# Decode attention of a hybrid decoder step: value pages become the stationary operand in full fp32

## The reference

```python
s = einsum('bqhcd,bkhcd->bhcqk', q, k_all) * ATTN_SCALE      # c: two halves of 64
p = softmax(s over the 1024 past and 4 new tokens)
w = p[:, :, 0] - lam * p[:, :, 1]                             # (8 heads, 4 queries, tokens)
out = einsum('bhqk,bkhe->bqhe', w, v_all)                     # per head: 4 queries x 128
```

## Time and profile before

| what | value |
|---|---|
| median of the runs | 1901.7 us |
| the profiled execution | 1898.74 us, its span 1896.6 us |
| decode, keys of sequence 0 (from the first transpose) | 1485.2 to 1510.7 us |
| decode, seven turns | 1510.7 to 1748.4 us |
| decode, values of sequence 7 | 1748.4 to 1774.3 us |
| output phase | 1778.7 to 1896.6 us |
| PE busy, mean granted clock over the span | 90%, 0.94 |

### The profile page before, as it was taken

How to read it: one execution, slowest core, us unless ns; L and a number is a source line. 1 busy time by engine, 2 the same in 40 slices (tenths; PEclk the granted TensorE clock), 3 DMA queues, 4 the chain that set the end, 5 groups by cost and what they waited for, 6 DMA issues and landing times. The chain is left out here.

```text
span 1896.6 us, 31172 instructions
## 1 busy us (share of the span) xinstructions
PE 1703.2 (90%) x9243; PEld 1384.7 (73%) x9243; DVE 1042.4 (55%) x2696; ACT 839.5 (44%) x1994; POOL 320.4 (17%) x814
## 2 busy tenths in 40 slices
PE   4299999999999997997999999999999588887798
PEld 3287887878788785777878778778788466665476
DVE  4534445444443444344777767767766466676443
ACT  5244434333343332243555545555545366665322
POOL 1011212212121120010122221221222012111101
PEclk8699999999999997998999999999999789898799
DMA  5123050340413103132211211211100567767713
GB/s 154 36 56 72 22 92 2 90 81 11 92 14 78 27 11 135 52 129 63 61 56 40 65 50 42 58 54 44 39 23 26 200 228 259 272 227 237 263 58 110
DMA packets 164757, 171.97 MB, mean 91 GB/s; under 512 B 14634, under 2 KB 133834, under 8 KB 164658
## 3 DMA queue, kind: packets, MB, share of 16 engines
q1 hardware_dynamic: 161538, 170.78, 30.6%
q10 hardware_dynamic: 3120, 0.01, 0.1%
HBM read 141.85 MB, written 28.91 MB: 90 GB/s over the span
## 5 line engine op out<-in xcount | busy, mean ns | idle before, releaser
L1016 PE MATMUL PS<-WH,XH 128*128 128x512 f32 x512 | 212.5, 415 | 0.0
L1016 PE MATMUL PS<-WH,XL 128*128 128x512 f32 x512 | 201.9, 394 | 0.0
L1016 PE MATMUL PS<-WL,XH 128*128 128x512 f32 x512 | 201.9, 394 | 0.0
L1997 PE MATMUL PS<-W,XH 128*128 128x512 f32 x384 | 123.8, 403 | 0.0
L2423 PE MATMUL PS<-cst,RAW 128*128 128x128 f32 x512 | 87.3, 322 | 40.5 <-DVE XL L2330 34.9
L1751 ACT ACTIVATE WORK<-PD,WORK 128x896 f32<-128x896 f32 (+7 forms) x128 | 94.9, 741 | 62.7 <-DVE WORK L1918 57.6
L1016 PEld LDWEIGHTS PS<-WH,XL 128*128 128x128 f32 x512 | 96.2, 188 | 22.8
L2423 PEld LDWEIGHTS PS<-cst,RAW 128*128 128x128 f32 x512 | 68.5, 165 | 58.7 <-DVE XL L2330 42.6
L1016 PEld LDWEIGHTS PS<-WH,XH 128*128 128x128 f32 x512 | 96.7, 189 | 19.8
L1016 PEld LDWEIGHTS PS<-WL,XH 128*128 128x128 f32 x512 | 96.8, 189 | 17.1
L2330 DVE TENSOR_TENSOR XL<-PS,XH 128x512 fp32r<-128x512 f32 x128 | 83.9, 684 | 38.2 <-ACT XH L2251 38.1
(11 more groups left out here) (361 smaller groups left out, 4575.4 us busy)
## 6 DMA issues: line engine op xcount, KB each, us to landing
RAW<-in_cache_k SPq DMA_DIRECT2D x64, 512.0 KB, 4.7
WORK<-in_cache_v SPq DMA_DIRECT2D x64, 512.0 KB, 4.6
RAW<-in_w_in_a SPq DMA_DIRECT2D x40, 512.0 KB, 7.0
out<-WORK SPq DMA_DIRECT2D x16, 512.0 KB, 3.0
out<-RAW SPq DMA_DIRECT2D x16, 512.0 KB, 3.2
RAW<-in_w_in_b SPq DMA_DIRECT2D x60, 128.0 KB, 2.3
RAW<-in_w_kv SPq DMA_DIRECT2D x56, 128.0 KB, 2.3
WORK<-d_G SPq DMA_DIRECT2D x8, 528.0 KB, 12.1
```

The lines of the kernel that those rows point to most:

```text
L1016: last = nc.tensor.matmul(bank, x[:, k, tok(t, P)], wkvoz(w)[:, k, :], start=(k == i == 0), stop=(k == KT - 1 and i == 2))
L1997: last = nc.tensor.matmul(out, x[:, k, at(NT - 1 - s)], w[:, k, cols], start=(k == i == 0), stop=(k == KT - 1 and i == 2))
```

## The change

The values are no longer split. A page of values in plain fp32 is the stationary operand, 128 x 128 per head, and the moving operand is that head's four columns of `WS`. `OUT` is now 128 x 32 (turned: a column per query), is copied into `OT` once per turn, and after the last sequence eight transposes bring `OT` back, straight into the row block of `X1` that the output phase reads. `d_av`, its stores and the 16 reads are gone, and so are `AVS`, `WTS`, `VH`, `VL` and GpSimd's part. Values have six slots, of which pages 4 and 6 share one, and 5 and 7 another. The transposes of keys go round four banks, and `W` takes its place in that round. `PE_ORDER` and `ORDER` are new. The page table is loaded in an earlier phase, and the first loads of keys no longer wait for `pre`.

```diff
-            VB = take(4, D)
+            V_SLOT = (0, 1, 2, 3, 4, 5, 4, 5)
+            VB = take(6, D)
-            OUT = PD[0]
-            ORDER = ("Q", "K0", "E", "K1", "K2", "K3", "V0", "W", "K4", "V1", "R0", "V2", "K5", "V3", "K6", "V4",
-                     "R1", "V5", "V6", "K7", "V7", "L")
-            PE_ORDER = ("T0", "T1", "T2", "T3", "S0", "T4", "W", "S1", "T5", "V0", "V1", "V2", "T6", "S2", "V3", "T7",
-                        "V4", "V5", "V6", "S3", "V7", "N")
+            OUT = BK[4][:, 0:H * DS]
+            TURNS = [u for u in range(10)] + ["W"] + [u for u in range(10, 16)]
+            T_BANK = {u: BK[(0, 1, 7, 5)[n % 4]] for n, u in enumerate(TURNS)}
+            ORDER = ("Q", "K0", "E", "K1", "K2", "K3", "K4", "W", "R0", "K5", "K6", "K7", "R1", "L")
+            PE_ORDER = ("T0", "T1", "T2", "S0", "T3", "T4", "W", "S1", "V0", "T5", "V1", "V2", "T6", "V3", "V4", "T7",
+                        "S2", "S3", "V5", "V6", "V7", "N")
...
                     def values(i, p):
+                        if p < 4:
+                            wait(sp, av, PAGES * (i - 1) + p + 1)
+                        elif p < 6:
+                            wait(sp, av, PAGES * (i - 1) + p + 3)
+                        else:
+                            wait(sp, av, PAGES * i + p - 1)
...
                         def value(p):
-                            for j in range(2):
-                                for w in (VH, VL):
-                                    x = nc.tensor.matmul(OUT[0:64, j, :], WTS[:, p, :], w[p % 4][:, 512 * j:512 * j + 512],
-                                                         start=(p == 0 and w is VH), stop=False)
+                            pe.wait_ge(v_ld[V_SLOT[p]], 16 * (i + 1) if p < 4 else 16 * (2 * i + (p - 2) // 2))
+                            if p == 0:
+                                pe.wait_ge(wr, i + 1)
+                                wait(pe, avc, i)
+                            apart(pe)
+                            for h in range(H):
+                                x = nc.tensor.matmul(OUT[:, h * DS:(h + 1) * DS], VB[:, V_SLOT[p], h * P:(h + 1) * P],
+                                                     WS[:, p * TS + h * DS:p * TS + (h + 1) * DS],
+                                                     start=(p == h == 0), stop=False)
...
                     sequences(pe, body)
+                    pe.wait_ge(avc, DB)
+                    pe.wait_ge(wr, DB)
+                    for h in range(H):
+                        x = nc.tensor.transpose(BK[h // 4][0:TS, (h % 4) * P:(h % 4 + 1) * P], OT[:, h, :], ident)
```

More of the change, by code:

```diff
@@ L2176, in keys, with values, turn @@
                           .then_inc(k_ld[p % 4], 16)
[L2178 to L2185, removed]
-                        src = cache_v[page(sp, i * PAGES + p), :, :, :]
[L2187 to L2201, removed]
+                    def values(i, p):
+                        if p < 4:
[4 more added lines that the diff above has]
+                            wait(sp, av, PAGES * i + p - 1)
+                        src = cache_v[page(sp, i * PAGES + p), :, :, :]
+                        sp.dma_start(VB[:, V_SLOT[p], :], src.rearrange("a p h e -> (a p) (h e)"))\
+                          .then_inc(v_ld[V_SLOT[p]], 16)
+                    def turn(b):
                         for p in range(4, PAGES):
@@ L2209, in _ @@
                             values(b, p)
-                        store(b - 1)
+                    for p in range(PAGES):
+                        keys(0, p)
+                    for p in range(4):
+                        keys(1, p)
+                        values(0, p)
+                    sp.wait_ge(pre, 1)
+                    turn(1)
+                    with sp.Fori(2, DB - 1) as b:
+                        turn(b)
                     for p in range(4, PAGES):
@@ L2294, in body @@
                                 exponentials()
[L2295 to L2298, removed]
                         if values:
                             act.wait_ge(avd, i + 1)
-                            wait(act, d_avs, 16 * i)
-                            for j in range(2):
-                                last = act.activation(AVS[0:64, 512 * j:512 * j + 512], OUT[0:64, j, :], ACT.Copy)
-                            last.then_inc(avc, 1)
+                            act.activation(OT[:, :, bass.ds(i * DS, DS)], OUT.rearrange("p (h q) -> p h q", h=H), ACT.Copy)\
+                               .then_inc(avc, 1)
                     sequences(act, body)
+                    act.wait_ge(fin, 1)
+                    act.activation(X1[0:TS, NT, 0:512], BK[0][0:TS, :], ACT.Copy).then_inc(out, 1)
                 @block.vector
@@ L2397, in body @@
                             elif step == "W" and values:
-                                weights_low()
-                            elif step[0] == "V" and values and int(step[1]) % 4 < 3:
-                                v_low(int(step[1]))
+                                weights()
                     sequences(dve, body, links, 4)
+                    dve.wait_ge(fin, 1)
+                    v.tensor_copy(X1[0:TS, NT, 512:1024], BK[1][0:TS, :]).then_inc(out, 1)
                 @block.tensor
```

124 lines of the change are left out of this document (41 added, 83 removed).

## The result

The kernel became slower. Four runs of the changed kernel gave 2010.48 to 2015.28 us, median 2012.83; the kernel before, four runs on the same chip, 1902.51. The ratio is 1.0579, 95% interval 1.0562 to 1.0596: +110 us. The forecast was 2023 us, slower.

The account below looks back on a forecast made before the run. PE's own work bounds a turn, with some 4 us of bank waits and part of the transposes at half clock. 124 - 10.5 - 0.8 + 10.4 - 2 = +121 on 1896.6/1898.7 gives 2020, median 2023 us; range 1900 to 2060.

Parts of the forecast that it names:

- The clock stays full: Rival, 15%: value steps leave PE no idle gaps, so the clock holds through decode; 1917 us, or 1909, still slower.
- Loads cost what a transpose's load does: Rival, 8%: at full clock each value load costs 0.062 us, so a page takes 1.2 us; 1865 us, faster.
- Half clock nearly throughout: Rival, 5%: nearly all PE steps of a decode turn run at half clock, 63.6 us per turn; 2110 us.
- wait for page 7: Late in each turn PE waits 2.6 us for values page 7, issued after `V5` and landing 4.6 us later.
- `V` at full / half clock: PE's step for one page of values: sixteen loads plus semaphore step and passage, 2.0 us at full, 3.7 at half clock.
- a turn, `W` to `W`: One decode turn on PE was to take 51.7 us instead of 34.0: +17.7.
- sample rows to the first turn (32.0 before): Keys of sequence 0: earlier start, 3.2 us less, and a stretch of 18.2 instead of 25.5 us; together -10.5.
- the seven turns (237.7 before): Seven decode turns at +17.7 us each, +124, less 0.8 because the first starts at full clock.
- values of sequence 7 (25.9 before): The last stretch of decode, eight value pages at half clock: 36.3 instead of 25.9 us, +10.4.
- `OUT` to the next phase (4.4 before): End of decode: a short copy, eight transposes and two copies, about 2.4 us, replace mostly the `d_av` store: -2.
- The wait of `S0`: Before these scores in each turn: no wait counted, `S0` itself 1.95 us; ACT's and DVE's work taken as off PE's path.
- The first turn: The first decode turn was to start at full clock, unlike the later ones at half: -0.8 us.

## Why the prediction was right

*The rivals.* "The clock stays full" is refuted by the windows above: with four columns moved it fell in every turn of the changed kernel. "Loads cost what a transpose's load does" is refuted by 0.106 us per record at full clock. "Half clock nearly throughout" didn't come: the matmuls of `S3` take 299 ns on average, as at full clock (L2378, 288 columns). The Trainium skill, "TensorE: Matmul & The Clock Gate", section "HAM oscillation — how this bites in real kernels", puts a falling clock down to idle gaps of PE. That the clock fell behind the wait for page 7 with 64 columns is of that kind, though this wait, 2.79 us, is shorter than the gaps that the section speaks of. The fall within `V1` is not, since PE had no gap there: by that section alone the changed kernel would have kept its clock up to page 7.

*The terms.* The table sets the forecast beside the trace. The span went from 1896.6 to 2013.5 us, +116.9, where the sum said +121. That it comes so near is in part luck: the turns came 14 us below the forecast, and nearly 10 us of other terms came above it.

| step | forecast | trace of the changed kernel |
|---|---|---|
| `V` at full / half clock | 2.0 / 3.7 | 1.70 / 3.35 |
| `N` at half clock | 3.6 | 3.5 |
| wait for page 7 | 2.6 | 2.4 (19.3 in 8) |
| a turn, `W` to `W` | 51.7 | (1815.07 - 1519.63) / 6 = 49.2 |
| sample rows to the first turn (32.0 before) | -10.5 | 1505.83 - 1483.54 = 22.3: -9.7 |
| the seven turns (237.7 before) | +124 - 0.8 | 1852.94 - 1505.83 = 347.1: +109.4 |
| values of sequence 7 (25.9 before) | +10.4 | 1890.05 - 1852.94 = 37.1: +11.2 |
| `OUT` to the next phase (4.4 before) | -2 | 1894.79 - 1890.05 = 4.7: +0.3 |
| the phases around decode | 0 | +4.8 ahead of it, +0.9 behind |

The term that was mis-sized is a page of values. I multiplied the right distance (0.11 and 0.21) by sixteen and then added 0.2 and 0.25 us for the semaphore step and the passage. The trace shows no such time: from the start of one step to that of the next are sixteen distances and no more. That is 0.3 us for each of eight pages and 0.1 in `N`, 2.5 us per turn, as much as 51.7 - 49.2. But it is not all that differs. The wait of `S0`, 11.9 us in eight turns, stood at nothing, and the clock fell later than I had it: `V1` and `V2` took 5.8 us in the first turn, not 7.2. These two offset each other.

The first turn went the other way. I had let it begin at full clock and gain 0.8 us; it took 13.8 us to its `W`, and lost 4 us in two waits for DVE:

```profile
1509.98 1.25 PE L2364 MATMUL PS<-cst,RAW 128*128 128x128 f32 x8 [2.25 <-DVE XL L2281]
1513.02 0.58 PE L2378 MATMUL PS<-XH,WH 128*128 128x256 f32 x1 [1.78 <-DVE XL L2281]
```

DVE stands at that moment in the maximum and the shares of the sequence before (1.25, 0.76 us and small ones), which lie in its queue before the low parts. In later turns `V7`, `N` and two pages at half clock stand between `S3` and `T2`, and `T2` waits no more; `S0` still does (11.9 us in eight turns). I had written that ACT's and DVE's work is off PE's path once the banks don't wait. For banks that is true but for this first `T2`; `S0`, however, needs the low part itself, whatever the number of banks.

The end came 2.3 us above the forecast. I took the store to `d_av` for most of the 4.4 us, which no run shows. Now there is no store, and eight transposes at half clock, two copies and 2.64 us until the next phase's first transpose take as long (what those 2.64 us wait for isn't shown; in the run with 64 columns and eight slots they are 1.04):

```profile
1890.30 1.89 PE L2431 MATMUL PS<-cst,WORK 128*32 128x128 f32 x8 [0.29 <-ACT WORK L2254]
1892.23 0.68 DVE L2338 COPY Y_ROWS<-PS 32x512 f32<-32x512 f32 x1 [34.35 <-PE PS L2431]
1894.83 1.94 PE L1525 MATMUL PS<-cst,Y_ROWS 128*128 128x128 f32 x8 [2.64 <-PEq L2151]
```

The 4.8 us ahead of decode belong to this one execution: the sample's rows are turned at 1483.54, at 1478.73 in the profile of before, and at 1479.58 in the run with two banks, which has the same code up to there. The run with three banks alone, which has the code of the kernel before up to there, turns them at 1483.91.

*Where the +110 comes from.* Taken apart by the runs: 46 to 48 us hang on what is streamed alone (64 columns), 89 to 91 on that together with the wait for page 7, 98 when `N`, the order and 128 columns come in, though with three banks. The rest, some 12 us over the kernel before, is left at nearly full clock, as the price of the loads and of the wait that three banks leave, less the gain of the banks. How much of the 98 each edit would have alone isn't told apart: they act through one clock, and their gains don't add. Nor was the end part of the change run by itself.

## What to carry to other kernels

Before you make the large operand stationary and the small one moving, multiply the number of loads by the distance of two load-bound records (0.106 us for 128 columns in full fp32, at full clock), and set it against what the streaming form costs. Then ask in which stretch little would be streamed: there the same loads can take twice as long, and everything that stands next to them too. If such steps can't be avoided, move padding with them, keep waits away from them, and put them singly between dense ones, which helped here on average though not in every turn. And take what is useful by itself without the rest: here the third bank, 15 us; the early start gained nothing that is clear of noise.

## What the runs showed that I had not expected

- A PE that was busy without a gap fell to half clock, in `V1`, with matmuls of four columns, and stayed there in windows in which it was busy for 3.40 of 3.40 us. With 64 columns, 1.74 instead of 1.70 us per page, it did not fall in these steps.
- The clock depended on its past: with 64 columns it held 1.00 from `V0` to `V6` in the turns but stayed at 0.50 when the values began there (3.45 us per page, in three runs). With 128 columns it came back from 0.50 within these values, after some 6 us in one run (13.89 us for six pages) and some 13 in the other.
- Moving columns that nobody reads costs next to nothing behind such loads: at full clock a page takes 1.70 us with four columns, 1.74 with 64, 1.78 with 128 (1520.33 - 1518.55 in that run).
- One change of order among PE's steps was worth 21 to 28 us, with the same instructions.
- Fewer subtractions on DVE did not pay: GpSimd's 2.4 us per page, in place of DVE's 1.27, made PE wait 15.8 us and the kernel 9 to 11 us slower.
